# Two weight blocks split early into the query buffer, and a new order of splits and norm steps, in a two-block transformer kernel

## The reference

```python
def rms_norm(x, gain):
    xf = x.astype(jnp.float32)
    y = xf * lax.rsqrt(jnp.mean(xf * xf, axis=-1, keepdims=True) + EPS)
    return (y * gain.astype(jnp.float32)).astype(x.dtype)
...
for i in range(DEPTH):
    h = rms_norm(x, norm_gains[i])
    ...                       # mixer(h): h @ w_in, attention, then (o * silu(z)) @ w_out
    x = x + y
...
h = h + merged @ w_out[l]
hn = rmsnorm(h, norm_ffn_g[l])
h = h + (jax.nn.silu(hn @ w_ffn_gate[l]) * (hn @ w_ffn_up[l])) @ w_ffn_down[l]
```

## Time and profile before

| | |
|---|---|
| median of 3 runs | 816.3 us (816.01 to 816.52) |
| the profiled execution | 816.29 us, of which the span of the profile is 814.1 us |
| TensorE matmul busy | 786.1 us, 97% of the span |
| weight load, VectorE, ScalarE, GpSimd busy | 687.7, 552.7, 425.8, 112.4 us |
| mean granted TensorE clock | 0.998 of full speed |
| DMA | 120.74 MB, 148 GB/s mean |

### The profile page before, as it was taken

One profiled execution on the slowest core, in us unless ns is written; L12 is line 12 of the kernel. 1 busy time (PEld: TensorE's weight loads), 2 busy tenths in 40 slices (PEclk: granted clock), 3 DMA queues, 4 the chain that ended last, 5 costly groups with the idle time before them and its releaser, 6 DMA issues.

```text
span 814.1 us, 13250 instructions
## 1 busy us (share of the span) xinstructions
PE 786.1 (97%) x5154; PEld 687.7 (84%) x5154; DVE 552.7 (68%) x910; ACT 425.8 (52%) x832; POOL 112.4 (14%) x108
## 2 busy tenths in 40 slices
PE   7999989998999899999999999999998999999996
PEld 4788987776898678999988999899986888888885
DVE  6897977747987664446636667886866665666665
ACT  5447557735548544446436445564444544545453
POOL 1334024501625220000000000011001000000000
PEclk9999999999999999999999999999999999999999
DMA  8756311133532335553442543435554557564641
GB/s 303 212 165 207 113 44 54 53 130 115 181 129 105 109 123 166 180 172 105 155 136 71 168 145 116 144 106 171 179 194 135 178 172 247 176 205 158 214 146 52
DMA packets 93105, 120.74 MB, mean 148 GB/s; under 512 B 8490, under 2 KB 69347, under 8 KB 93044
## 3 DMA queue, kind: packets, MB, share of 16 engines
q1 hardware_dynamic: 92176, 117.68, 44.4%
q0 software_dynamic: 432, 1.57, 0.5%
q10 hardware_dynamic: 436, 0.65, 0.2%
HBM read 118.85 MB, written 1.05 MB: 147 GB/s over the span
## 4 chain that ended last, share of the span: by engine, by line
PE 86%; DVE 7%; issue 2%; ACT 2%; POOL 2%; DMA 1%; ACTq 0%; POOLq 0%; DVEq 0%
PE banks L429 20%; PE banks L431 19%; PE banks L430 19%; PE banks L473 8%; PE banks L475 4%; DVE w_lo L1640 2%; PE banks L1045 1%; PE banks L436 1%; PE banks L435 1%; PE banks L534 1%; PE banks L616 1%; ACT w_hi L1196 1%; PE banks L570 1%; PE banks L582 1%; PE banks L659 1%
## 5 line engine op out<-in xcount | busy, mean ns | idle before, releaser
L1640 DVE TENSOR_TENSOR w_lo<-raw,w_hi 128x1024 fp32r<-128x1024 f32 x216 | 270.5, 1262 | 105.9 <-ACT w_hi L1196 105.3
L1196 ACT CAST w_hi<-raw 128x1024 fp32r<-128x1024 f32 (+1 forms) x217 | 225.7, 1047 | 150.5 <-PE banks L431 109.1
L429 PE MATMUL banks<-h,w_hi 128*128 128x256 f32 (+1 forms) x512 | 149.6, 292 | 0.3 <-DVE w_lo L1640 0.3
L430 PE MATMUL banks<-h,w_hi 128*128 128x256 f32 (+1 forms) x512 | 145.5, 284 | 0.0
L431 PE MATMUL banks<-h,w_lo 128*128 128x256 f32 (+1 forms) x512 | 144.9, 283 | 0.0
L429 PE MATMUL banks<-w_hi,h 128*128 128x512 f32 (+1 forms) x288 | 114.7, 398 | 7.1 <-DVE h L1647 4.2
L431 PE MATMUL banks<-w_hi,h 128*128 128x512 f32 (+1 forms) x288 | 112.4, 390 | 0.0
L430 PE MATMUL banks<-w_lo,h 128*128 128x512 f32 (+1 forms) x288 | 112.0, 389 | 0.0
L473 PE MATMUL banks<-h,w_hi 128*128 128x512 f32 x288 | 99.1, 392 | 0.0
L429 PEld LDWEIGHTS banks<-h,w_hi 128*128 128x128 f32 x512 | 96.1, 188 | 2.4 <-issue 1.7
L430 PEld LDWEIGHTS banks<-h,w_hi 128*128 128x128 f32 x512 | 96.4, 188 | 0.2
(11 more groups left out here) (344 smaller groups left out, 1336.9 us busy)
## 6 DMA issues: line engine op xcount, KB each, us to landing
raw<-in_w_in SPq DMA_DIRECT2D x24, 1024.0 KB, 5.2
raw<-in_a_w_in SPq DMA_DIRECT2D x13, 1024.0 KB, 5.1
raw<-in_w_ffn_gate SPq DMA_DIRECT2D x11, 1024.0 KB, 5.3
raw<-in_w_ffn_up SPq DMA_DIRECT2D x11, 1024.0 KB, 5.4
raw<-in_w_ffn_down SPq DMA_DIRECT2D x11, 1024.0 KB, 4.9
raw<-in_b_w_in SPq DMA_DIRECT2D x9, 1024.0 KB, 5.3
raw<-in_w_gate SPq DMA_DIRECT2D x8, 1024.0 KB, 5.7
raw<-in_a_w_out SPq DMA_DIRECT2D x4, 1024.0 KB, 5.0
```

Of the source, the lines that this page charges most:

```text
L429: mm(o, lh, rh, start=start, stop=False)
L430: mm(o, lh, rl, start=False, stop=False)
L1196: nc.scalar.copy(split(w_hi, s), rawsub(s)[0]).then_inc(S["hi_ready"], 1)
L1640: V.tensor_tensor(split(w_lo, s), rawsub(s)[0], split(w_hi, s).bitcast(F), ALU.subtract).then_inc(S["lo_ready"], 1)
```

## The change

There are three parts, all in the three seams (stages 1 to 3).

1. Blocks W0 and W1 of each seam, called AHEAD, are split into the query buffer: high parts into `o2_hi`, low parts into `o2_lo`, W0 into its first half and W1 into its second. Both may be made once block s0 + 3 is used up (`slot_free`). All other blocks keep the ring, numbered without the six AHEAD blocks, so that W2 and W3 wait for blocks s0 + 4 and s0 + 5 (before: s0 + 6 and s0 + 7), and W4 and W5 for s0 + 6 and s0 + 7 (before: W0 and W1). From the block behind W5 on, each waits for the same block as before.
2. The order on ScalarE: W0 and W1 are made before the first stats, W2 and W3 next, then the high parts of `h` of tile 0, then the stats of tile 1, then W4 and W5, and the high parts of tile 1. The order on VectorE: W0 and W1 before the first residual; the low parts of `h` of tile 0 directly behind the residual of tile 1's first half; W2, the sum of tile 1, W3, `norm_apply` and `norm_lo` of tile 1, and W4 and W5 last.
3. The sum of squares plus EPS of tile 1 moves from GpSimd to VectorE (`norm_sum`) in stages 1 to 3; GpSimd keeps it in stage 0.

No instruction is added besides: as many splits, stats and matmuls as before.

```diff
+        AHEAD = [first[n] + 8 + i for n in ("a_out", "b_out", "c_out") for i in range(2)]
+        ringed = [s for s in range(NSUB) if s not in AHEAD]
+        ring_at = {s: k for k, s in enumerate(ringed)}
+
+        def slot_free(s):
+            if s in AHEAD:
+                return s - 4 - AHEAD.index(s) % 2
+            return ringed[ring_at[s] - RING] + 1 if ring_at[s] >= RING else 0
+
         def split(ring, s):
             _, a, b = rawsub(s)
+            if s in AHEAD:
+                i = AHEAD.index(s) % 2
+                t = (o2_hi if ring is w_hi else o2_lo)[:, 4 * i:4 * i + 4, :].rearrange("p a n -> p (a n)")
+                return t[:, 0:a * b].rearrange("p (a b) -> p a b", a=a)
...
-            return ring[:, s % RING, 0:a * b].rearrange("p (a b) -> p a b", a=a)
+            return ring[:, ring_at[s] % RING, 0:a * b].rearrange("p (a b) -> p a b", a=a)
...
-                    if s >= RING:
-                        act.wait_ge(S["sub_used"], s - RING + 1)
+                    if slot_free(s):
+                        act.wait_ge(S["sub_used"], slot_free(s))
...
             def norm_stage(n, s0):              # ScalarE
 
-                split_hi_to(s0 + 4 + RING)
+                split_hi_to(s0 + 10)
                 norm_stats(n, 0, 0)
                 norm_stats(n, 0, 1)
-                split_hi_to(s0 + 4 + RING + 1)
+                split_hi_to(s0 + 12)
+                norm_hi(n, 0)
                 norm_stats(n, 1, 0)
-                split_hi_to(s0 + 4 + RING + 2)
-                norm_hi(n, 0)
-                split_hi_to(s0 + 4 + RING + 3)
                 norm_stats(n, 1, 1)
-                split_hi_to(s0 + 4 + RING + 4)
+                split_hi_to(s0 + 14)
                 norm_hi(n, 1)
...
+            def norm_sum(n, tt):
+                c = 2 * n + tt
+                dve.wait_ge(S["n_sq"], 4 * n + 2 * tt + 2)
+                V.tensor_scalar(st_var[:, c:c + 1], st_ss[:, n, tt, 0:1], st_ss[:, n, tt, 1:2], EPS, ALU.add, ALU.add).then_inc(S["n_ss"], 1)
...
             def norm_stage(n, s0):              # VectorE
 
-                split_lo_to(s0 + 4 + RING)
+                split_lo_to(s0 + 10)
                 residual(n, s0, 0, 0)
                 residual(n, s0, 0, 1)
                 norm_apply(n, 0)
                 residual(n, s0, 1, 0)
-                split_lo_to(s0 + 4 + RING + 1)
                 norm_lo(n, 0)
                 residual(n, s0, 1, 1)
-                split_lo_to(s0 + 4 + RING + 3)
+                split_lo_to(s0 + 11)
+                norm_sum(n, 1)
+                split_lo_to(s0 + 12)
                 norm_apply(n, 1)
-                split_lo_to(s0 + 4 + RING + 4)
                 norm_lo(n, 1)
+                split_lo_to(s0 + 14)
...
             def norm_rstd(n, tt):               # GpSimd
 
                 c = 2 * n + tt
-                if tt:
+                if tt and n == 0:
                     pool.wait_ge(S["n_sq"], 4 * n + 4)
                     G.tensor_scalar(st_var[:, c:c + 1], st_ss[:, n, tt, 0:1], st_ss[:, n, tt, 1:2], EPS, ALU.add, ALU.add).then_inc(S["n_ss"], 1)
```

More of the change, by code:

```diff
@@ L295, in rawsub @@
             return t[:, :, j * b // subs:(j + 1) * b // subs], a, b // subs
+        AHEAD = [first[n] + 8 + i for n in ("a_out", "b_out", "c_out") for i in range(2)]
[5 more added lines that the diff above has]
+            return ringed[ring_at[s] - RING] + 1 if ring_at[s] >= RING else 0
         def split(ring, s):
             _, a, b = rawsub(s)
+            if s in AHEAD:
+                i = AHEAD.index(s) % 2
+                t = (o2_hi if ring is w_hi else o2_lo)[:, 4 * i:4 * i + 4, :].rearrange("p a n -> p (a n)")
+                return t[:, 0:a * b].rearrange("p (a b) -> p a b", a=a)
             if s == first["a_gl"]:
                 lo = 0 if ring is w_hi else 48
-                return w_hi[:, s % RING, 0:2 * a * b].rearrange("p (a b) -> p a b", a=a)[:, :, lo:lo + b]
-            return ring[:, s % RING, 0:a * b].rearrange("p (a b) -> p a b", a=a)
+                return w_hi[:, ring_at[s] % RING, 0:2 * a * b].rearrange("p (a b) -> p a b", a=a)[:, :, lo:lo + b]
+            return ring[:, ring_at[s] % RING, 0:a * b].rearrange("p (a b) -> p a b", a=a)
         def zb_log(hh):
@@ L795, in _ @@
             pe.wait_ge(S["tq_c"], 4)
-            both = w_hi[:, s % RING, 0:96 * KT].rearrange("p (a b) -> p a b", a=KT)
+            both = w_hi[:, ring_at[s] % RING, 0:96 * KT].rearrange("p (a b) -> p a b", a=KT)
             for kt in range(KT):
@@ L1637, in split_lo_to @@
                     dve.wait_ge(S["hi_ready"], s + 1)
-                    if s >= RING:
-                        dve.wait_ge(S["sub_used"], s - RING + 1)
+                    if slot_free(s):
+                        dve.wait_ge(S["sub_used"], slot_free(s))
                     V.tensor_tensor(split(w_lo, s), rawsub(s)[0], split(w_hi, s).bitcast(F), ALU.subtract).then_inc(S["lo_ready"], 1)
@@ L1653, in norm_apply @@
                 if tt == 0:
-                    dve.wait_ge(S["n_sq"], 4 * n + 2)
-                    V.tensor_scalar(st_var[:, c:c + 1], st_ss[:, n, 0, 0:1], st_ss[:, n, 0, 1:2], EPS, ALU.add, ALU.add).then_inc(S["n_ss"], 1)
+                    norm_sum(n, 0)
                 if n:
```

## The result

The changed kernel takes 809.84 us (median of 4 runs, 809.63 to 810.68) against 816.4 us before (816.01 to 816.52): a ratio of 0.9922, 95% interval 0.991 to 0.9934. The forecast was 809.9 us, range 808.3 to 811.6. The profiled execution took 809.84 us, of which the span is 807.9; before it was 814.1.

What follows compares the result with a forecast made beforehand. TensorE sets the time, its matmuls busy 786.1 of 814.1 us. Seam stalls of 7.87 us, less 2 x 0.68 (D) and 0.1 (longer matmuls), give 6.4: 816.3 - 6.4 = 809.9 us, range 808.3 to 811.6.

Steps and rivals of the forecast that it cites:

- The stalls that could be won: TensorE's waits in the three seams, A, B and C together: 7.87 us, the most the change can take from them.
- A: TensorE's stall at the start of each seam's first panel, for the low part of `h`: 4.26 us in all, forecast gone.
- B: TensorE's stall at the first panel's second block, for W1, in stages 1 and 3: 0.92 and 0.93 us, forecast gone.
- C: TensorE's stall behind the transposes of tile 1, for W3, in stages 1 and 3: 0.88 us each, forecast gone.
- D: New stall: tile 1's transposes wait for `xn`, GpSimd's power being held by W3's low part; 0.68 us in stages 1 and 3.
- Rival 2: A stays in part, `norm_hi` beginning 0.6 us later; each stage keeps 0.4 + 0.24: 812.2 us; chance 9 in 100.
- W0 and W1 early: Both split once s0 + 3 is used; first residual to about 180.7, second stays at 181.03; B gone, 1.85 us.
- rival 4: ScalarE blocked at W0 by a late load; 14 us loads in every seam would give 818.4 us; chance 2 in 100.
- Rival 1: No hold on GpSimd, or a short one: the power precedes W3's low part, D is 0.15, 808.7 us; chance 17 in 100.
- The prediction's other estimate for D: Release about 115 ns behind VectorE's end and the whole power after it: D an estimated 0.9 us.
- The sign to look for: Profile sign of D: two waits of the transposes for `xn`, stages 1 and 3 alone, 0.3 to 0.5 us each.
- rival 3: Seam gain given back behind it, in work needing other engines; half lost, more in stage 1: 812.3 us; chance 6 in 100.

## Why the prediction was right, point by point

- **The stalls that could be won, 7.87 us.** Right: none of A, B and C is left in the seams, and no other stall came out from behind them but D.
- **A, gone by a margin of 0.17 us.** Right. Two experiments that delay the low part of `h` by 0.34 and 0.54 us bring back 0.16 and 0.37 in stage 1: a margin of 0.18 and 0.17 (0.16 and 0.15 in stage 3). Rival 2 needed a gap that did not exist. Its price was also too high: it added 0.24 to each stall, the term for the idle time in brackets, where its own way from start to start adds 0.08. The experiment that held `h` back lost 0.45 to 0.53 us for each A, not 0.64.
- **W0 and W1 early, at no cost.** Right. The first residual went from 178.25 to 180.31 and the second kept its releaser. ScalarE had no wait for a load there, so rival 4 had no ground; a load late enough to test it was not tried. Its 0.7 us a seam does not follow from its own terms, 14 - 6.1 - 3.0 - 0.3 - 3 = 1.6. The room for the second residual, stated as 0.3 us, was 0.34 in stage 1 and 0.21 in stage 3.
- **D, 0.68 us in stages 1 and 3, nothing in stage 2.** Right, 0.70, 0.74 and nothing. The power ended 0.41 us behind the low part of W3, where I had 0.35, and lay inside the bounds of 0.09 and 0.57. Rival 1, no hold, is out by the 1.47 us and by the power of 0.56 once the neighbour is gone. The rule of the Trainium skill ("SBUF — State Buffer", section "Who interferes with whom") holds here: 0.57 against 1.47 us. The prediction's other estimate for D takes the release at 115 ns and the whole power behind it; the page states that figure in its section "A bandwidth-pool intuition that's wrong (but worth ruling out)", for a DMA whose descriptors GpSimd writes. The estimate was too high. By its own terms it is 1.0 us and not the 0.9 that the prediction gives, as 0.115 + 0.57 is 0.34 more than the 0.35 behind the 0.68. Measured are 0.41 us behind VectorE for the power and 0.09 for the sum, so a part of the instruction seems to be over before the hold begins. The sign to look for was a little off too: TensorE's waits for `xn` are listed with 0.25 and 0.29 us, not 0.3 to 0.5, because the listed length of the matmul before hides 0.16 of each.
- **Part 3, the moved sum.** The prediction named the 1.50 us that leave GpSimd and the hold that comes to the power, but did not set one against the other. The experiment does: 0.41 us in all by the stalls.
- **W4 and W5, and what follows each seam.** Right: the other waits of TensorE are as they were, and rival 3 found nothing, since the distance to the kernel before moves by less than 0.1 us in each stretch behind a seam.
- **The small errors.** The seams give 6.43 us against 6.4 forecast; the span says 6.2, and the rest is the load at the start. The 0.1 us for a longer matmul behind each D had no ground: the matmul behind the transposes is listed with 0.47 or 0.48 us with a stall before it and without (185.78 in the earlier trace rows, 186.08 and 193.24 above). It made up for a D that was 0.04 too small on average. That the difference of the medians (6.56) agrees so closely has some luck in it, since the runs of one kernel spread by half a microsecond or more.

## What to carry to other kernels

Free buffers are not early work: an instruction queue written out by hand must also ask for the data earlier, and here the buffer alone gave 0.0 us, the order 3.7, both 6.5. When a short instruction on GpSimd is listed as long, look at what VectorE ran at the same time before moving it, because its successor may inherit the wait. And where TensorE is 97% busy, read stalls from start to start: the stall of 0.16 us showed no idle time in the list.

## What the runs showed of the hardware

A GpSimd instruction on 128x1 is stretched from 0.31 to 1.50 us (sum) or from 0.56 to 1.47 us (power) while VectorE runs low parts of weights, which read two inputs from SBUF. The held instructions ended 0.09 us (sum) and 0.41 us (power) behind VectorE's.

The hold works in both directions. Outside the seams GpSimd multiplies tiles of 128x512, which takes 1.04 us when nothing holds it (at 68.82 or 250.85, for example). Three places of the changed kernel:

```profile
32.60 3.21 DVE L1651 TENSOR_TENSOR w_lo<-raw,w_hi 128x1024 fp32r<-128x1024 f32 x2
32.72 2.02 POOL L2388 TENSOR_TENSOR ar<-ar,small 128x512 f32<-128x512 f32 x1 [0.47 <-DVE ar L1704]
...
245.83 3.02 POOL L2403 TENSOR_TENSOR ar<-ar,small 128x512 f32<-128x512 f32 x2 [1.00 <-DVE small L1859]
245.97 1.98 DVE L1651 TENSOR_TENSOR w_lo<-raw,w_hi 128x1024 fp32r<-128x1024 f32 x1
...
251.93 2.05 DVE L1651 TENSOR_TENSOR w_lo<-raw,w_hi 128x1024 fp32r<-128x1024 f32 x1
```

At 245.83 and 251.85 a multiply starts first, and the low part that starts 0.14 or 0.08 us behind it takes 1.98 or 2.05 us instead of 1.22. At 32.72 a multiply starts 0.11 us behind a low part and takes 2.02 us, 0.90 of them behind the end of that low part. Then it is VectorE that is held: the second low part takes 2.07 us, and the pair 3.21 instead of 2.35. So GpSimd can get in between two low parts without a gap. The sum in the earlier trace rows did not; it was held through both. It had started 0.20 us ahead of the second low part, the multiply 1.03 us ahead. This suggests that the sum asked too late, but no run varies it. Beside VectorE's reduction of a bank, a multiply of this size takes 1.04 us (at 120.00), so not every instruction of VectorE holds GpSimd; the experiments themselves vary only whether a low part stands there.
